# Stationary-weight products of a decoder block: a panel's upper-half products first, then its lower-half products

## The reference

```
x = x + hybrid_mixer(rms_norm(x, g1))     # 6 projections (w_in), 4 retention heads, RG-LRU, then w_out
x = x + cross_attend(rms_norm(x, g2), rms_norm(mem, gm))   # wq, wk, wv, wo; 4 heads, 256 memory rows
x = x + conv_ffn(rms_norm(x, g3))         # w_up to 2 x 5632, causal conv of 3 taps, silu(a) * b, w_down
return rms_norm(x, g_final)
```

## Time and profile before

| | |
|---|---|
| median of 3 runs | 1525.22 us |
| span of the profiled execution | 1522.5 us |
| PE busy | 1507.2 us, 99% |
| PE weight loads busy | 1286.4 us, 84% |
| VectorE busy | 1060.5 us, 70% |
| ScalarE busy | 806.3 us, 53% |
| DMA | 288.88 MB, 190 GB/s |

### The profile page before, as it was taken

How to read it: one execution, slowest core, us unless ns; L and a number is a source line. 1 busy time by engine, 2 the same in 40 slices (tenths; PEclk the granted TensorE clock), 3 DMA queues, 4 the chain that set the end, 5 groups by cost and what they waited for, 6 DMA issues and landing times.

```text
span 1522.5 us, 23967 instructions
## 1 busy us (share of the span) xinstructions
PE 1507.2 (99%) x7844; PEld 1286.4 (84%) x7844; DVE 1060.5 (70%) x1552; ACT 806.3 (53%) x1160; POOL 2.9 (0%) x9
## 2 busy tenths in 40 slices
PE   8999999999999999999999999999999999999997
PEld 6888888888888888888888888888888888888886
DVE  5756666788887555444568777777777777777776
ACT  5644477744555545334566454454545545454554
POOL 0000000000000000000000000000000000000000
PEclk9999999999999999999999999999999999999999
DMA  9766655565557555444546555555555555555553
GB/s 325 254 190 216 206 179 184 199 202 166 171 165 263 179 194 166 138 152 154 192 160 200 194 190 182 193 180 191 191 183 192 183 188 193 190 182 192 181 194 138
DMA packets 80314, 288.88 MB, mean 190 GB/s; under 512 B 8928, under 2 KB 10464, under 8 KB 79376
## 3 DMA queue, kind: packets, MB, share of 16 engines
q1 hardware_dynamic: 76320, 276.33, 54.8%
q10 hardware_dynamic: 3456, 8.64, 1.6%
q0 software_dynamic: 496, 3.34, 0.6%
HBM read 286.18 MB, written 2.10 MB: 189 GB/s over the span
## 4 chain that ended last, share of the span: by engine, by line
PE 98%; DVE 1%; DMA 0%; ACT 0%; SPq 0%; issue 0%
PE ps L255 97%; DMA raw<-in_stream 0%; PE ps L310 0%; DVE vm L1298 0%; DVE xres L1308 0%; DVE wlo L836 0%; PE ps L433 0%; PE ps L382 0%; ACT scr L813 0%; DVE xres L1271 0%; SPq L212 0%; DVE wlo L890 0%; ACT vm L826 0%; ACT whi L553 0%; DVE vm L1317 0%
## 5 line engine op out<-in xcount | busy, mean ns | idle before, releaser
L255 PE MATMUL ps<-xT,whi 128*128 128x512 f32 x2304 | 817.4, 399 | 0.0
L836 DVE TENSOR_TENSOR wlo<-raw,whi 128x1024 fp32r<-128x1024 f32 x516 | 622.8, 1221 | 126.4 <-ACT whi L513 118.9
L513 ACT ACTIVATE whi<-raw 128x1024 fp32r<-128x1024 f32 x516 | 531.9, 1051 | 229.8 <-PE ps L255 222.3
L255 PE MATMUL ps<-xT,wlo 128*128 128x256 f32 x2304 | 646.2, 280 | 0.0
L255 PEld LDWEIGHTS ps<-xT,whi 128*128 128x128 f32 x2304 | 432.7, 188 | 105.3
L255 PE MATMUL ps<-whi,mixT 128*128 128x512 f32 x1472 | 461.7, 392 | 7.4 <-DVE wlo L894 5.6
L255 PEld LDWEIGHTS ps<-xT,wlo 128*128 128x128 f32 x2304 | 435.1, 189 | 0.9
L255 PEld LDWEIGHTS ps<-whi,mixT 128*128 128x128 f32 x1472 | 277.2, 188 | 66.8 <-DVE mixT L885 5.6
L255 PE MATMUL ps<-wlo,mixT 128*128 128x512 f32 x736 | 287.2, 390 | 0.0
L528 ACT ACTIVATE hl<-ps 128x256 f32<-128x256 f32 x160 | 61.5, 384 | 273.4 <-PE ps L255 273.3
L854 DVE TENSOR_TENSOR tmp<-ps,hl 128x256 f32<-128x256 f32 x160 | 67.8, 424 | 180.0 <-ACT hl L528 180.0
(11 more groups left out here) (165 smaller groups left out, 599.5 us busy)
## 6 DMA issues: line engine op xcount, KB each, us to landing
raw<-in_stream SPq DMA_DIRECT2D x519, 512.0 KB, 3.3
xres<-in_xin ACTq DMA_DIRECT2D x2, 1024.0 KB, 6.8
scr<-in_xt_in ACTq DMA_DIRECT2D x8, 256.0 KB, 3.5
xres<-in_xin POOLq DMA_DIRECT2D x1, 2048.0 KB, 10.4
out_x<-vm SPq DMA_DIRECT2D x4, 512.0 KB, 3.1
kT<-in_memt_in SPq DMA_DIRECT2D x2, 512.0 KB, 8.7
vbuf<-in_memin ACTq DMA_DIRECT2D x1, 1024.0 KB, 8.5
gel<-in_memin ACTq DMA_DIRECT2D x1, 1024.0 KB, 8.3
```

Of the source, the lines that this page charges most:

```text
L255: return nc.tensor.matmul(o, l, r, start=start, stop=stop, skip_group_check=True)
L513: A(whi[:, 2 * pr + s, :], raw[:, 2 * pr + s, :], ACT.Copy).then_inc(hi_done, 1)
L836: V.tensor_tensor(wlo[:, 2 * pr + s, :], raw[:, 2 * pr + s, :], f32(whi[:, 2 * pr + s, :]), ALU.subtract).then_inc(lo_done, 1)
```

## The change

In `narrow`, the loop over a panel's eight tiles, which issues the `whi` matmul and the `wlo` matmul of a tile one behind the other, becomes two loops: eight `whi` matmuls, then eight `wlo` matmuls. The calls in `at` stay in the first loop. The start flag is still on the first matmul of the 16 tiles, the stop flag and the raising of `panels_used` on the last. `wide` is not touched.

```
--- before.py
+++ after.py
@@ -264,9 +264,10 @@
                         kk = 8 * s + k
                         if kk in at:
                             at[kk]()
-                        w = slice(k * P, (k + 1) * P)
-                        mm(acc, whi[:, 2 * pr + s, w], lhs[:, kk].rearrange("p a b -> p (a b)"), kk == 0, False)
-                        last = mm(acc[:, :T], wlo[:, 2 * pr + s, w], lhs[:, kk, 0, :], False, kk == KT - 1)
+                        mm(acc, whi[:, 2 * pr + s, k * P:(k + 1) * P], lhs[:, kk].rearrange("p a b -> p (a b)"), kk == 0, False)
+                    for k in range(8):
+                        kk = 8 * s + k
+                        last = mm(acc[:, :T], wlo[:, 2 * pr + s, k * P:(k + 1) * P], lhs[:, kk, 0, :], False, kk == KT - 1)
                     last.then_inc(panels_used, 1)
```

## The result

The changed kernel takes **1517.4 us** (median of four runs, 1517.17 to 1518.00) against 1525.4 for the kernel before (four runs). The ratio is 0.9949 with a 95% interval of 0.9935 to 0.9963: 8 us faster, between 5.6 and 9.9. The forecast was 1520, 5 us faster, and its own range was 1512 to 1526. The span of the profiled execution fell by 7.1 us, from 1522.5 to 1515.4; that execution of the kernel before was a quick one (the spans of nine later runs of it have a median of 1523.3 us), which is why the spans differ by less than the medians.

A forecast was written before the change was run, and what follows sets the result against it. PE, busy 99% of the span, bounds the kernel through matmul start distances. Panels save 6.4 us, calls lose 1.5: net -4.9, span 1522.5 to 1517.6, plus 2.7 carried over gives 1520 us; own range 1512 to 1526, wider range 1497 to 1545.

The forecast's parts named there:

- PE's rate is all there is: Whole kernel: PE is busy 99% of the span, so time can come only from the rate at which matmuls follow.
- Eight hi at 232.5 ns, 1860: The panel's eight whi matmuls (512 columns) in a row: 232.5 ns each, 1860 ns, between bounds of 227 and 236.
- Eight lo at 117, 936: The panel's eight wlo matmuls (256 columns) in a row: 117 ns each, 936 ns, today's recorded mean.
- the lower end: Lower bound for a wlo matmul's slot: 109 ns, taken from eight transposes, each with its load.
- Today's panel at 2816: A panel of eight alternating whi and wlo pairs before the change: 8 x 352 = 2816 ns, in 320 panels.
- 1.5 us for the calls: Calls from `at` come earlier in the panel, so PE stalls at index 7: 1.5 us lost in sum.
- Index 7: Transposes ahead of the query product: 0.88 us earlier against 0.35 slack, stall 0.5 to 0.6; ahead of FFN, shared with `row_of(2)`.
- index 14: Wait behind more matmul time since index 7 than before; claimed to cost nothing new.
- Both blocks clean: Rival for `narrow`'s panels: the loss belongs to alternating alone, whi 227 ns, wlo 113, total 1496 us; chance 0.20.
- Nothing moves: Rival for `narrow`'s panels: each load beside a 256-column stream is charged, eight in either order; 1523 to 1531 us, chance 0.20.
- Load-bound lo: Rival for the wlo block: chained loads start late, 126 ns or more a slot, whi still 232.5; 1543 us, chance 0.25.
- point of decision, 119 ns: Break-even wlo slot: from 119 ns on the slower rival decides, with the whi block at 1860 ns.

The follow-up runs named there:

- groups of two: Changed kernel with two whi then two wlo matmuls in turn within a panel, instead of eight and eight: ratio 0.9935, median 1515.8 us, against the kernel before.
- groups of eight and four: Eight is the changed kernel, span 1515.4 us; four is the changed kernel with four whi then four wlo matmuls in turn, span 1518.8 us.
- the short loads: 64 stationary columns instead of 128: wlo matmuls in the changed kernel, span 1503.3 us; whi matmuls except each product's first in the kernel before, 1493.4 us.

## Why the prediction held, step by step

- **PE's rate is all there is.** Right: same engines, clock and counts; only the distances between starts changed.
- **Eight hi at 232.5 ns, 1860.** Measured 230, 1840. The row I took, 512s behind a narrow stretch, showed the right thing, a lateness left by what went before. But in it the first slot followed the 353 rhythm (241, then 238); behind a lo block it is 233. 20 ns too much.
- **Eight lo at 117, 936.** Measured 119, 953: 17 ns too little. Today's recorded lo slot was a mean over a rhythm of 113, 117 and 120 in which part of the price stood in the hi slot; in a row the lo settles at 120. The two errors cancelled, panel 2796 against 2793, and that is luck: with the lo right and the hi as I had it, the panel would have been 2813 and the forecast 5 us later. The transposes that I took for "the same weight load" at the lower end are not: eight of their loads take 0.91 us with starts 109 ns apart, so one is recorded with some 0.14 us, a load of `whi` with 0.19. The sum did not use that bound.
- **Today's panel at 2816.** The mean over the panels without calls is 2819. With 2793 that is 26 ns a panel, 8.3 us, where the sum had 6.4. Of the missing 2 us one half is this term, the other the 3 ns left over from hi and lo.
- **1.5 us for the calls.** In place and sign right, and not by its own working. Index 7 lost 0.46 us in each of two stretches; index 14, which I had at nothing, lost 0.3 in each, since the tiles that it waits for hang on VectorE's splits and not only on matmul time since index 7; and `row_of(2)`, for which I had the rest, waits no longer than before, as the stalls ahead of it gave VectorE the time. 2 x 0.78 less the 2 x 0.07 and 0.2 lost there before is about 1.2. The gates kept a slack of 0.5 us (expected 0.33) and never waited.
- **What I had not followed up**: the two stretches that the earlier trace rows show at 346 ns a pair (2773 a panel) are those after a norm, so the change, with 2793, made their panels slower. My mean of 352 held this as an average only; it is why those stretches lose some 0.35 us each on top of their stalls instead of gaining.
- **Rivals.** "Both blocks clean" (1496) fell to 230 and 119 ns. "Nothing moves" counted right, eight loads beside lo streams in either order, but the price of one depends on what follows it. "Load-bound lo" named the mechanism that the short loads confirmed, and had its size wrong: 120 instead of 126. Its point of decision, 119 ns, was met exactly; the change won because the hi block was cheaper than the 232.5 on which that point rested.

The forecast of 1520 stands 2.9 us from the measured median: 2 from the panels, 0.3 from the calls, the rest from the 2.7 us that I carried over. That was the distance from one quick execution's span to the median of other runs; in every run that has both, the time is 1.7 to 1.9 us above its own span.

## What to carry to other kernels

Where PE is busy all the time, read the distances between starts one by one: a loss of 13 ns at every second matmul made 2% of this kernel and shows in no busy share. A matmul whose stream is as short as the load of the next weights is the place to look; halving the load, in a kernel that leaves out half the output rows of these matmuls, tells in one run whether the load is to blame. Reordering only moves such a loss about: try the small group sizes instead of assuming that longer blocks are better, and follow each wait that hangs in the reordered loop to the end of its chain.

## What the runs showed of the hardware

- With fp32r operands a settled stream of 512 columns took 227 ns and one of 256 took 113, half of it, when the load beside it had 64 columns: the overhead over 2.4 GHz is a sixteenth, and not a fixed time for each matmul.
- Whole loads of `whi` or `wlo` (128 weight columns) in a row followed each other every 112 ns beside 192 moving columns, every 120 beside 256, and every 227 beside 512 without any loss.
- One whole load beside a 256-column stream delays up to five matmuls after it, 27 ns in all when these are 512 wide, 14 when they alternate.
- A fixed sequence has several stable rhythms, 353 and 346 ns a pair in one execution of one kernel, and it changed behind the transposes and waits after a norm, but not behind the gates' fp32 matmuls. What fixes the rhythm is open, and with it why groups of two beat groups of eight and four. Open too is the loss at 288 and 320 columns; at 320 it was as large with half the load.
